# Loads issued one stage earlier, key turns placed between other steps, and two tiles of output products moved into the recurrence's last part

## What is computed

```python
h = rms_norm(x, norm1_g) * (1 + scale1) + shift1
p = h @ w_in                                   # one projection, columns split among three mixers
y_rwkv = rwkv_mix(...)                         # a recurrence with a state per head (4 heads)
y_gmlp = gmlp_mix(...)                         # gating inside chunks of 128 tokens
y_sb   = sb_sweep(q, k_all, v_all, ...)        # attention, 8 heads; sampled tokens also read
                                               # 8 pages of 128 cached keys and values each,
                                               # picked by page_table
x  = x + gate1 * (concat([y_rwkv, y_gmlp, y_sb]) @ w_out)
h2 = rms_norm(x, norm2_g) * (1 + scale2) + shift2
x  = x + gate2 * hier_moe(h2)                  # router picks a group, then 2 experts of 4
y  = rms_norm(x, final_g)
```

## Time and profile before

| what | value |
|---|---|
| median of 3 runs | 1580.27 us (1579.11 to 1586.65) |
| profiled execution: its own time | 1573.23 us |
| profiled execution: span, first to last instruction | 1571.5 us |
| TensorE busy | 1343.4 us, 85% of the span |
| VectorE, ScalarE, GpSimd busy | 624.0, 424.9, 131.9 us |
| mean granted TensorE clock | 0.939 of full speed |
| moved by DMA | 191.66 MB, mean 122 GB/s |

### The profile page before, as it was taken

The page is one execution under the profiler, slowest core; times in us unless marked ns, Lnnn a source line. Parts: engine busy times, 40 slices in busy tenths (PEclk is TensorE's granted clock), DMA queues, the critical chain, the costliest instruction groups (busy, mean ns, idle before and its releaser), DMA issues. The chain is left out here.

```text
span 1571.5 us, 29011 instructions
## 1 busy us (share of the span) xinstructions
PE 1343.4 (85%) x10641; PEld 774.5 (49%) x10641; DVE 624.0 (40%) x1214; ACT 424.9 (27%) x860; POOL 131.9 (8%) x338
## 2 busy tenths in 40 slices
PE   5999799989999999957877999789962999999945
PEld 3554455445353535335546888634432555555522
DVE  4202427613626272733333455523344222222217
ACT  3101134113636372723331233201120111111113
POOL 0100110000101010100000000040000111010031
PEclk9999899999999999969997999989985999999978
DMA  9202032721010100066743000080003658846775
GB/s 363 73 0 74 21 93 94 270 83 42 1 41 1 41 1 15 1 215 231 244 167 122 16 4 4 5 233 37 34 34 153 242 199 310 300 161 239 270 247 198
DMA packets 87505, 191.66 MB, mean 122 GB/s; under 512 B 17995, under 2 KB 41042, under 8 KB 77811
## 3 DMA queue, kind: packets, MB, share of 16 engines
q1 hardware_dynamic: 74004, 158.09, 28.9%
q0 software_dynamic: 6256, 20.71, 3.9%
q10 hardware_dynamic: 7152, 11.55, 2.3%
HBM read 163.01 MB, written 27.31 MB: 121 GB/s over the span
## 5 line engine op out<-in xcount | busy, mean ns | idle before, releaser
L2671 PE MATMUL ex_ps_g<-all_mT,ex_xt 128*64 128x256 f32 x1344 | 157.3, 388 | 16.9 <-DMA all_mT<-in_exp_wu 15.5
L2671 PEld LDWEIGHTS ex_ps_g<-all_mT,ex_xt 128*64 128x64 f32 x1344 | 97.6, 139 | 64.2 <-issue 12.6
L1692 PE MATMUL at_ps_z<-all_hT,mix_v_g 128*128 128x363 f32 (+1 forms) x384 | 122.3, 477 | 4.4 <-PEq L105 4.4
L2298 PE MATMUL op_ps_o<-all_hT,op_m_t 128*128 128x512 f32 x256 | 116.1, 609 | 7.6 <-POOL op_m_t L2278 7.6
L577 PE MATMUL rp_ps<-all_hT,rp_w 128*128 128x384 f32 (+1 forms) x336 | 109.0, 480 | 8.3 <-DMA rp_w<-in_w_in 8.3
L1841 DVE TENSOR_SCALAR at_zc<-at_ps_z,at_bias 128x512 f32<-128x512 f32 (+3 forms) x96 | 54.5, 613 | 136.2 <-PE at_ps_z L1708 135.4
L1692 PEld LDWEIGHTS at_ps_z<-all_hT,mix_v_g 128*128 128x128 f32 x384 | 73.6, 193 | 51.8 <-issue 11.1
L341 PE MATMUL fr_big<-all_mT,all_hT 128*128 128x256 f32 (+3 forms) x288 | 94.9, 493 | 3.0 <-DVE all_hT L394 3.0
L577 PEld LDWEIGHTS rp_ps<-all_hT,rp_w 128*128 128x128 f32 x336 | 63.5, 193 | 55.1 <-issue 11.7
L2688 PE MATMUL ex_ps_y<-all_hT,ex_hid_T 128*64 128x512 f32 x336 | 80.5, 599 | 2.0 <-issue 1.2
L2298 PEld LDWEIGHTS op_ps_o<-all_hT,op_m_t 128*128 128x128 f32 x256 | 48.7, 194 | 66.0 <-issue 58.0
(11 more groups left out here) (478 smaller groups left out, 2032.5 us busy)
## 6 DMA issues: line engine op xcount, KB each, us to landing
all_mT<-in_exp_wg SPq DMA_DIRECT2D x17, 1024.0 KB, 4.9
all_mT<-in_exp_wu SPq DMA_DIRECT2D x17, 1024.0 KB, 8.0
all_hT<-in_exp_wd SPq DMA_DIRECT2D x17, 1024.0 KB, 8.0
all_hT<-in_cache_k SPq DMA_DIRECT2D x64, 256.0 KB, 4.2
sa_v<-in_cache_v SPq DMA_DIRECT2D x64, 256.0 KB, 5.0
slot_rows<-ex_y ACTq DMA_DIRECT2D x84, 128.0 KB, 5.4
mix_v_g<-in_w_mod SPq DMA_DIRECT2D x8, 1024.0 KB, 5.1
rp_w_mod<-in_w_mod SPq DMA_DIRECT2D x8, 1024.0 KB, 5.7
```

The source lines that it names most:

```text
L1692: last = nc.tensor.matmul(third(x_, c), w[:, x_, k, :], hT[:, k, lo:hi], start=(k == 0), stop=(k == KT - 1))
L2298: last = nc.tensor.matmul(ps_o[0:m, u, lo:lo + 512], m_t[:, u, k, 0:m], w[:, k, lo:lo + 512], start=(k == 0), stop=(k == KT - 1))
L2671: final = nc.tensor.matmul(ps_g[rows, u, 0:DE], xt[:, k, HALVES[u]], w1[:, u, x_, k, :], start=(k == 0), stop=(k == KT - 1))
```

## The change

1. `rwkv_project`'s first two weight blocks are loaded by SyncE in `gated_mlp`, behind that stage's own loads. The buffers live longer (`keep["rp_w"]`).
2. The page table and the keys of sequences 0 and 1 are loaded by SyncE in `attention`, after the last projection has read `hT` and ahead of the last store of keys. `sampled_attention`'s SyncE then begins with the values of sequences 0 and 1, and its loop starts at sequence 2.
3. In `sampled_attention` the turns of sequence 0's keys stand between the new tokens' steps on TensorE, and their copies between the new tokens' steps on ScalarE.
4. The products of `w_out` with prompt tiles 0 and 1 stand on TensorE between the steps that are left after the last `turn` of `rwkv_chunks`. The eight banks are shared by `rwkv_chunks` and `out_project` (`keep["banks"]`); products go to banks 0 and 1 or 5 and 6.
5. In `out_project` GpSimd's copies into `m_t` are gone: the products read `mT`. TensorE's loop is written out, and in it the first half of product(n + 2), or `product_sampled`, stands ahead of turn(n) and add(n - 1).

```diff
+def out_product(nc, keep, n, half, ks):
+
+    m, lo = rows_of(n), half * 512
+    for k in ks:
+        last = nc.tensor.matmul(out_banks(keep, n % 2)[0:m, lo:lo + 512], keep["mT"][:, k, n * P:n * P + m],
+                                keep["w_out"][:, k, lo:lo + 512], start=(k == 0), stop=(k == KT - 1), skip_group_check=True)
+    return last
...
-                load(0)
-                load(1)
                 sp.dma_start(carried[:, :], T["state_rwkv_shift"]).then_inc(s["small_loaded"], 16)
...
+                def projected(n, half, ks=range(KT)):
+
+                    if ks[0] == 0:
+                        pe.wait_ge(keep["w_out_loaded"][half], 16)
+                        pe.wait_ge(g["normed"], STEPS_OF_NORM * (n + 2))
...
+                n = TURNS - 1
+                of_u(n, 0)
+                without_u(n, 0)
+                projected(0, 0, range(0, 4))
+                with_u(n, 0)
+                mean_of(n - 1)
+                projected(0, 0, range(4, KT))
+                of_u(n, 1)
+                without_u(n, 1)
+                projected(0, 1, range(0, 4))
+                with_u(n, 1)
+                square_sum_of(n - 1)
+                projected(0, 1, range(4, KT))
+                mean_of(n)
                 pe.wait_ge(g["s_kept"], 2 * (TURNS - 1) + 1)
                 for f in range(2):
                     last = by_head(ones(2)[:, f, :], S[:, 0, f, :], I2)
                 last.then_inc(g["prompt_turned"], 1)
-                square_sum_of(TURNS - 1)
+                projected(1, 0)
+                square_sum_of(n)
+                projected(1, 1)
...
+                for n in range(2):
+                    at = PROJECT_ORDER[n] * P
+                    sp.dma_start(keep["rp_w"][:, n, :, :], T["w_in"].rearrange("(k p) n -> p k n", p=P)[:, :, at:at + P]).then_inc(keep["rp_w_loaded"][n], 16)
                 sp.wait_ge(did, LN_STEPS)
...
+                sp.dma_start(keep["table"][:, :], T["page_table"]).then_inc(keep["table_loaded"], 16)
+                sp.wait_ge(keep["table_loaded"], 16)
+                sp.wait_ge(g["proj_done"], 6 * PAIRS)
+                for u in range(2):
+                    load_pages(sp, T["cache_k"], keep["pages"][:, u, :, :], pages_of(sp, keep["table"], u), keep["k_loaded"][u])
                 store(PAIRS - 1)
...
-                each(sp, SB, load)
+                for b in range(2):
+                    load_values(b, b, pages_of(sp, table, b))
+                with sp.Fori(1, SB // 2) as i:
+                    for u in range(2):
+                        load(i * 2 + u, u)
...
+                new_scores()
+                turn(0, 0, 0, 0)
+                new_sums()
+                turn(0, 0, 0, 1)
+                new_values()
                 for half in range(2):
-                    turn(0, 0, 0, half)
                     score(0, 0, half)
...
-                keep_keys(0)
+                keep_keys(0, range(0, 2))
+                new_logs()
+                keep_keys(0, range(2, 6))
+                new_weights()
+                keep_keys(0, range(6, NPAGE))
...
-                def stage(n, u, r):
-                    m = rows_of(n)
-                    pool.wait_ge(s["product_done"], n + 1)
-                    nc.gpsimd.tensor_copy(m_t[:, u, :, 0:m], mT[:, :, bass.ds(n * P, m)]).then_inc(s["staged"], 1)
...
+                pe.sem_inc(s["product_done"], 2)
+                pe.wait_ge(s["r_padded"], 1)
+                for n in range(NT + 1):
+                    u = n % 2
+                    if n + 2 < NT:
+                        product(n + 2, 0)
+                    elif n + 2 == NT:
+                        product_sampled()
                     turn(n, u)
-                    if not first:
+                    if n:
                         add(n - 1)
...
+                    if n + 2 < NT:
+                        product(n + 2, 1)
                     route(n, u)
```

More of the change, by code:

```diff
@@ L485, in rwkv_project @@
         s = {x_: ph.sem(x_) for x_ in names.split()}
-        w_loaded = [ph.sem(f"w_loaded{u}") for u in range(2)]
         mod_loaded = [ph.sem(f"mod_loaded{u}") for u in range(2)]
@@ L906, in rwkv_chunks @@
         S_out, S_out_prompt = UVm, U_s
-        bank = [ph.ps(f"bank{x_}", [P, 512]) for x_ in range(8)]
+        bank = [keep["banks"][:, x_, :] for x_ in range(8)]
         def pairs(b):
@@ L1879, in _, with pages_of, load_pages @@
                             keep_run(j, steps[i - 3][0])
+def pages_of(eng, table, b):
+    return [eng.value_load(table[0:1, bass.ds(b * NPAGE + n, 1)], min_val=0, max_val=79) for n in range(NPAGE)]
+def load_pages(eng, cache, dst, pages, loaded):
+    for n, page in enumerate(pages):
+        eng.dma_start(dst[:, n, :], cache[bass.ds(page, 1), :, :].squeeze(0)).then_inc(loaded, 16)
 def sampled_attention(nc, T, keep):
@@ L3028, in build @@
                 keep["ks"] = kv.sb("ks", [P, SH // 2, NS])
+                keep["table"], keep["table_loaded"] = kv.sb("table", [1, SB * NPAGE], I32), kv.sem("table_loaded")
+                keep["pages"] = keep["hT"][:, :, :].rearrange("p k t -> p (k t)")[:, 0:2 * NPAGE * SBW].rearrange("p (u n c) -> p u n c", u=2, n=NPAGE)
+                keep["k_loaded"] = [kv.sem(f"k_loaded{u}") for u in range(2)]
                 with Phase(nc, "mix") as mix:
@@ L3035, in build @@
                     front(nc, T, keep)
+                    keep["rp_w"], keep["rp_w_loaded"] = mix.sb("rp_w", [P, 2, KT, P]), [mix.sem(f"rp_w_loaded{u}") for u in range(2)]
                     gated_mlp(nc, T, keep)
@@ L3039, in build @@
                 sampled_attention(nc, T, keep)
+            products = Phase(nc, "oc")
+            keep["banks"] = products.ps("banks", [P, 8, 512])
             rwkv_chunks(nc, T, keep)
```

157 lines of the change are left out of this document (66 added, 91 removed).

## The result

The changed kernel takes 1592.37 us in the median of 18 runs, the kernel before 1582.24 us in 18 runs beside it. The ratio is 1.0064 with a 95% interval of 1.0047 to 1.0081: slower by 10.1 us (7.4 to 12.8). The forecast was +4.8 us; the time lies inside the range, 1574 to 1595, but 0.64% above the kernel before, just outside the 0.5% to either side that I gave the most weight.

The account below looks back on a forecast made before the run. TensorE, busy for 85% of the span, was taken as the bound. Weights -4.2, keys -9 and products +18 gave +4.8 us: 1573.2 to 1578.0 profiled, about 1585 as median against 1580.3, range 1574 to 1595.

Parts of the forecast that it names:

- The products, +18: Recurrence's end and `out_project`: two tiles of output products moved into the recurrence make the kernel 18 us slower, bounds 10 to 21.
- The 7.1 us at the drain: End of `out_project`'s loop: with the sampled product ahead of turn(6) and add(5), norm(7) starts 7.1 us later, uncovered.
- a wait hidden under products: Start of `out_project`: VectorE waits 18.65 us for the router's weights, unfelt by TensorE while it has products until 1058.4.
- the sampled product as the cover of norm(7): End of `out_project`, kernel before: TensorE runs the sampled product for 7.09 us while VectorE does norm(7).
- The weights of `rwkv_project`, -4.2: Start of `rwkv_project`: with its first weights loaded ahead, TensorE starts with the barrier, 4.2 us sooner, bounds 2.5 to 4.3.
- the half clock for the first products "as now": Start of `rwkv_project`: the pause still leaves TensorE at half clock for the first products, as before the change.
- The keys, -9: `sampled_attention`: keys turned in TensorE's waits between the new tokens' steps save 9 us, bounds 6 to 10.7.
- the row at 696: `sampled_attention`, kernel before: a profile row with clock 1.00 from 696 on, taken as reason for the upper end, -9.
- my lower bound of 6: `sampled_attention`: the keys' gain with the low clock throughout, 6 us instead of 9.
- the rival in which the queue gives it back: `sampled_attention`: SyncE issues sequence 2's keys only after values(0), so the -9 is lost: +13.8, 1594; chance 8%.
- The rival with the router's weights early: Start of `out_project`: router's weights release VectorE at about 10 instead of 19.6, total -4.8, 1575.5; chance 12%.
- The likeliest case, within 0.5%: Whole kernel: time within 0.5%, 7.9 us, of the kernel before, given 60%.

## Why the prediction was right and where it was not

**The products, +18, measured +20.1 (15.8 to 24.2).** Right in mechanism and in nearly every piece. Forecast: stage start 18.2 us later, VectorE released 19.6 after it, TensorE idle for 22, 2.2 lost at the low clock, 6 waited at turn(7). In the trace: 18.1 (`out_project`'s first VectorE rows, 1045.06 and 1026.98), 19.5, 23.10, 9.42 - 7.13 = 2.3, and 5.70. The 7.1 us at the drain were 7.3 in the run that undid it. What I called a wait hidden under products, and the sampled product as the cover of norm(7), were the two places that decided; with both mended the same products cost nothing, and probably gain.

**The weights of `rwkv_project`, -4.2, measured -3.5 (0.8 to 6.2 faster).** The start moved as said. What was wrong is the half clock for the first products "as now", a cost that I put at nothing: the clock rose later, and the first product took 0.6 us longer in the mean of the profiles. The stage as a whole took 1.0 us longer (149.7 against 148.8). The wait for modulation weights at its end, which rival B of that run named, differs by 0.3 us between the two groups, less than it varies inside each.

**The keys, -9, measured -6.2 (3.5 to 8.7).** The order of steps came as listed, `turn_scores` at 692.80 where I had 693. The step that failed is the size: from the row at 696 I took the upper end, with the clock rising early. In the run with this edit alone the second sum and the new values still took 2.07 us. Counted over all profiles, values(0) stands 36.8 us behind the stage's first product with the edit and 44.2 without, and the stage lasts 152.3 and 158.9 us: 6.6 to 7.4 us less, near my lower bound of 6, which was the sum without the clock. That it passes to the stage's end through SyncE's queue was right, and the rival in which the queue gives it back was wrong.

**The rival with the router's weights early.** I priced it at 9.6 us, as if nothing but these weights held VectorE. The row shows only the last of several waits; the next one ended 2 to 3 us before it. The Trainium skill, page "DMA: Bandwidth & Descriptors", section "Anatomy of one DMA — SWDGE (gpsimd) path", fits one transfer on GpSimd's queue by about 2.0 us plus its bytes at 436 GB/s, which is an estimated 3.2 us for 512 KB and 2.2 for 64 KB. No run here agrees in this place, on SyncE's queue with other loads under way: in the changed kernel 64 KB took 16.7 us and 512 KB 5.4 to 15.0.

**The sum.** +4.8 against +10.1 (7.4 to 12.8): 0.7 from the weights, 2.8 from the keys and 2.1 from the products, all the same way, so no error cancelled another. Together they are 5.6 us, about the 5.3 that are missing. The likeliest case, within 0.5%, was therefore just missed at 0.64%, and the range was wide enough. Each term lies inside the interval of its own run but for the keys, whose 9 is just outside.

## What to carry to other kernels

A block of work that is moved away leaves the waits it had covered: list every wait that ran beside it, and for a wait on several operands the second and third that are due, before counting the idle time that it fills. One wait for all operands at a stage's start costs as much as the latest of them; waiting for each where it is first read gave back 7.7 us of the stage here with no load moved. And a gain at a stage's start has to be followed to the same stage's end: here the first product, at a lower clock for longer, took part of it.

## What the runs showed that I had not expected

- At `out_project`'s start the size alone doesn't give the time to landing. In the changed kernel three rows of 512 KB, issued within 1.4 us of each other, took 5.4, 9.5 and 15.0 us, the later the longer; 64 KB behind them took 16.7, and 3 MB behind those 17.6. With the router's transfers moved to another stage and the 3 MB issued 8 us sooner, the shift row took 16.1 us.
- One profile of each kernel is a poor measure of a few us. In 14 profiled executions the stages from `experts` on, the same in all, lasted 395.4 to 404.5 us, `sampled_attention` without the edit 155.1 to 161.5, and with it 148.5 to 155.1. The kernel before had the shortest of its kind and the changed kernel nearly the longest of its own (154.9); that is why the pair of profiles seemed to show no gain there. `out_project` on the other hand lasted 147.4 to 147.7 us in all six profiles with its old order.
